# Moving the MLP's operands and the weight buffers within the SBUF partition of a two-layer trunk kernel

## The chip, the cores and the metric

The kernel runs on one core of one Trainium2 chip. The metric is device time in microseconds (us) of one execution; the median of three runs is quoted. The change alters no instruction, no size and no wait, only the addresses at which some buffers lie in each partition of the on-chip memory SBUF.

## The reference

Two layers over 512 tokens of width 1024, float32. Cut to what matters here:

```python
for l in range(2):
    z = rms_norm(x, g[0]) @ w_in[l]                 # 1024 x 3328: attention, gating unit, retention
    x = x + rms_norm(mix @ w_out[l], g[1])          # mix: the three head groups, from z
    # cross-attention into 256 memory tokens: x_wq, x_wkv, x_wo, all 1024 wide
    x = x + rms_norm(memory_attention(rms_norm(x, g[2]), mem_n, x_wq[l], x_wkv[l], x_wo[l]), g[3])
    h = rms_norm(x, g[4])
    f = jnp.square(jax.nn.relu(h @ w_up[l])) @ w_down[l]   # 1024 -> 4096 -> 1024
    x = x + rms_norm(f, g[5])
```

## The kernel before

Every large product is done on TensorE with three matmuls for one product of 128 x 128 by 128 x N: both operands are split into a high and a low part of type fp32r, and `three_passes` (L546 to L548) adds high*high, high*low and low*high into one PSUM tile of `proj`. The first operand of a matmul is the stationary one (loaded by an instruction of its own, LDWEIGHTS), the second one moves through the array, one column after another.

Weights come in blocks of four chunks of 128 rows by 512 columns (1 MB). SyncE loads a block into one of two slots of `w_raw` (L450, L512, L521), ScalarE copies it to `w_hi` (L905), VectorE subtracts to `w_lo` (L1149), and TensorE waits for `w_lo_done` before the block's first tile. `block_tile` then does, for each of the block's tiles, 4 chunks x 3 passes = 12 matmuls, in one of two modes:

- "tok": the activations are stationary and the weights move (output rows are tokens). Per layer: `va`, `qc`, `kc`, `vc`, `gc` with 384 columns; `uv`, `out0`, `out1`, `wo0`, `wo1` with 512 columns, 4 tiles each; `vm0`, `vm1` with 512 columns and 2 tiles.
- "feat": the weights are stationary and the activations move (output rows are features). Per layer: `qa`, `ka` (3 tiles of 512 columns), `qx0`, `qx1` (4 tiles of 512), `km0`, `km1` (4 tiles of 256).

Each job has 2 blocks. The activations of these jobs are `hT_hi`/`hT_lo` (normalised, transposed rows), for `km` and `vm` `memT_hi`/`memT_lo`. The MLP follows in four groups a layer, each `up0`, `up1` ("feat", from `hT` into `proj`, then relu, square and split into `uT_hi`/`uT_lo`, L1070, L1419, L1073, L1423) and `dn0`, `dn1` ("tok", `uT` stationary, 512 columns), 2 blocks of 4 tiles each. `first_up` does the first `up0` of a layer in two halves of 256 columns.

SBUF buffers are allocated in the order of the `sb(...)` calls, per partition: `xs`, `hT_hi`, `hT_lo`, `w_raw`, `w_hi`, `w_lo`, `ys` of 16 KiB each, `gains` 12, `hs` 8, `squares` 4, then some 15.5 KiB of small ones (`ident` first), then the arena of 56 KiB. Counted from the start of `xs`, `hT` lies at 16 to 48 KiB, the three weight buffers at 48 to 96 KiB, and the arena begins at 151.5 KiB. In the arena `part(name, kib, ...)` places buffers that take turns: among others `uT_hi` at 0, `uT_lo` at 16, `relu` at 32, `memT_hi` at 32 and `memT_lo` at 40 KiB, and the attention's rows.

Small products (scores, transposes by `ident`, retention) go into the PSUM tensor `work` in plain float32, between the tiles of the jobs.

Of the kernel before, what the change touches and what calls it, by code (L numbers as in the profile page):

```python
# [8 lines left out]
F32R = mybir.dt.float32r  # L9
# [7 lines left out]
P = 128  # L17
DEPTH, S, D, MEM = 2, 512, 1024, 256
# [13 lines left out]
KC = D // P  # L32
BK = 4
# [33 lines left out]
WSLOTS = 2  # L67
# [172 lines left out]
def trunk(nc, x, mem, positions, norm_g, w_in, sgu_w, sgu_b, sgu_ln_g, sgu_ln_b, w_out,  # L240
          x_wq, x_wkv, x_wo, w_up, w_down, c_ident, c_logcount, c_upper, c_decay, c_inv, out):
    weights = {"w_in": w_in, "w_out": w_out, "x_wq": x_wq, "x_wkv": x_wkv, "x_wo": x_wo}
    with ExitStack() as ctx:
        def sb(name, shape, dt=F32):
            return ctx.enter_context(nc.sbuf_tensor(name, shape, dt))
# [2 lines left out]
        xs = sb("xs", [P, T, D])  # L248
        hT_hi = sb("hT_hi", [P, KC, S], F32R)
        hT_lo = sb("hT_lo", [P, KC, S], F32R)  # L250
        w_raw = sb("w_raw", [P, WSLOTS, BK, 512])
        w_hi = sb("w_hi", [P, WSLOTS, BK, 512], F32R)
        w_lo = sb("w_lo", [P, WSLOTS, BK, 512], F32R)
        ys = sb("ys", [P, T, D])
        gains = sb("gains", [P, 3, D])
        hs_start = nc.sbuf_base
# [42 lines left out]
        gn_var = sb("gn_var", [P, NH])  # L299
        gn_ve = sb("gn_ve", [P, NH])  # L300
        gn_rstd = sb("gn_rstd", [P, NH])


        KIB = 1024
# [3 lines left out]
        def part(name, kib, shape, dt=F32):  # L308
            return nc.alloc_sbuf_tensor_at(name, shape, dt, offset=arena_start + int(kib * KIB))
# [26 lines left out]
                        "e3": part("half_squares3", 48, [P, T, 512], BF16)}  # L336
        half_squares["e2"] = half_squares["e1"]

        uT_hi = part("uT_hi", 0, [P, KC, S], F32R)
        uT_lo = part("uT_lo", 16, [P, KC, S], F32R)  # L340
        relu = part("relu", 32, [P, 2, S])

        proj = ctx.enter_context(nc.psum_tensor("proj", [P, 4, 512], F32))
# [196 lines left out]
        def _(pe):  # L540
# [9 lines left out]
            def block_tile(b_slot, kb, mode, t, moving, hi, lo, cols, at=0):  # L550

                for k in range(BK):
                    c = kb * BK + k
                    first, last = c == 0, kb == KB - 1 and k == BK - 1
                    if mode == "tok":
                        r = slice(t * P, (t + 1) * P)
                        mm = three_passes(proj[:, t, 0:moving], hi[:, c, r], lo[:, c, r],
                                          w_hi[:, b_slot, k, 0:cols], w_lo[:, b_slot, k, 0:cols], first, last)
                    else:
                        r = slice(t * P, (t + 1) * P)  # L560
                        tokens = slice(at, at + moving)
                        mm = three_passes(proj[:, t, tokens], w_hi[:, b_slot, k, r], w_lo[:, b_slot, k, r],
                                          hi[:, c, tokens], lo[:, c, tokens], first, last)
                return mm
# [233 lines left out]
            def first_up(l):  # L798


                late_slots = ((1, 0), (1, 1))
                for half in range(2):
                    turned_in(l, ("n3", 2 * half + 1))
                    for kb in range(KB):
                        b = HEAD_BLOCKS + kb
                        if half == 0:
                            pe.wait_ge(w_lo_done, nth(w_lo_done, l, b + 1))
                        for t in range(4):
                            if half == 0 and kb == 0:

                                pe.wait_ge(gained, nth(gained, l, GAINED["e2", 1, t] + 1))
                            mm = block_tile(b % WSLOTS, kb, "feat", t, S // 2, hT_hi, hT_lo, 512, at=half * (S // 2))
                            if half:
                                mm.then_inc(tile_done, 1)
                            if half == 0 and (kb, t) in late_slots:
                                turn_normed(l, "n3", 2 + late_slots.index((kb, t)))

            def mlp_group(l, g, jobs=GROUP_JOBS, last=False):
                for name in jobs:
                    i = GROUP_JOBS.index(name)  # L820
                    for kb in range(KB):
                        b = HEAD_BLOCKS + KB * i + kb
                        pe.wait_ge(w_lo_done, nth(w_lo_done, l, g * GROUP_BLOCKS + (b + 1)))
                        for t in range(4):
                            if kb == 0:

                                if name == "up0":
                                    pe.wait_ge(added, nth(added, l, g * UP_TILES + (t + 1 - T)))
                                elif name in ("up1", "dn0"):
                                    pe.wait_ge(emptied, nth(emptied, l, g * UP_TILES + (HEAD_TILES + 4 * (i - 1) + t + 1)))  # L830
                                else:
                                    pe.wait_ge(added, nth(added, l, g * UP_TILES + (t + 1)))
                            if name == "dn0" and t == 0:

                                pe.wait_ge(hidden_lo, nth(hidden_lo, l, g * UP_TILES + 4 * (kb + 1)))
                            if i < 2:
                                mm = block_tile(b % WSLOTS, kb, "feat", t, S, hT_hi, hT_lo, 512)
                            else:
                                mm = block_tile(b % WSLOTS, kb, "tok", t, 512, uT_hi, uT_lo, 512)
                            mm.then_inc(tile_done, 1)  # L840
                            if last and name == "dn0" and kb == 1 and t < MT:
                                turn_normed(l, "memk", t)
# [45 lines left out]
        def _(act):  # L888
# [196 lines left out]
            with act.Fori(0, DEPTH) as l:  # L1085
                for b in range(HEAD_BLOCKS):
                    if b < HEAD_BLOCKS - 1:
                        head_split(l, b + 1)
                    before_block(l, b)
                    tiles = JOBS[b // KB][5]  # L1090
                    if b < HEAD_BLOCKS - 1:
                        for t in range(tiles):
                            if b % KB == KB - 1:
                                empty(l, b, t)
                            after_tile(l, b, t)
                    if b == FIRST_BLOCK["qx1"] + 1:
                        for j in range(2, XUNITS - 2):
                            x_step(l, j)

                for what, t in N3_ACT:  # L1100
                    if what == "e":
                        empty(l, HEAD_BLOCKS - 1, t)
                    elif what == "x":
                        act.wait_ge(x_ready, nth(x_ready, l, BRANCHED["e2", t] + 1))
                        sum_squares(l, ("n3", t), xs[:, t])
                    elif what == "h":
                        turn_hi(l, ("n3", t), hT_hi, t)
                    else:
                        split_hi(l, HEAD_BLOCKS + t)
                with act.Fori(0, GROUPS - 1) as g:  # L1110
                    mlp_group(l, g, False)
                    split_hi(l, HEAD_BLOCKS + GROUP_BLOCKS + 1, g=g)
                mlp_group(l, GROUPS - 1, True)
# [3 lines left out]
        def _(dve):  # L1117
# [332 lines left out]
            with dve.Fori(0, DEPTH) as l:  # L1450
                links = itertools.count(1)
                for b in range(HEAD_BLOCKS):
                    if b < HEAD_BLOCKS - 1:
                        head_split(l, b + 1)
                    before_block(l, links, b)
                    if b == HEAD_BLOCKS - 1:
                        continue
                    for t in range(JOBS[b // KB][5]):
                        after_tile(l, links, b, t)
                    if b == FIRST_BLOCK["out0"]:  # L1460
                        for t in range(MT):
                            norm_mem(l, "memv", t)
                    if b == FIRST_BLOCK["qx1"] + 1:
                        for j in range(2, XUNITS - 2):
                            x_step(l, links, j)

                for what, t in N3_DVE:
                    if what == "e":
                        gain(l, "e2", 1, t)
                    elif what == "x":  # L1470
                        update(l, "e2", t)
                    elif what == "n":
                        norm(l, ("n3", t), xs[:, t])
                    elif what == "h":
                        turn_lo(l, ("n3", t), hT_hi, hT_lo, t)
                    else:
                        split_lo(l, HEAD_BLOCKS + t)
                with dve.Fori(0, GROUPS - 1) as g:
                    mlp_group(l, g, False)
                    split_lo(l, HEAD_BLOCKS + GROUP_BLOCKS + 1, g=g)  # L1480
                mlp_group(l, GROUPS - 1, True)
                assert next(links) == DVE_LINKS + 1
# [137 lines left out]
```

## Time and profile before

| | |
|---|---|
| median of three runs | 1605.96 us (1603.81 to 1606.32) |
| span of the profiled execution, first to last instruction | 1603.6 us |
| median less span: what lies around it | 2.3 us |
| TensorE busy | 98% of the span, 8008 matmuls |
| VectorE, ScalarE, GpSimd busy | 44%, 36%, 11% |
| chain of work that ended last | 91% on TensorE |

The page gives for each engine its busy share; a matmul's record is longer than its share of the engine, since matmuls overlap, so the rate of TensorE is read from the start times of successive matmuls and not from their durations. In the page's and the trace's names, `proj<-hT_hi,w_hi` is a matmul into `proj` whose moving operand is `hT_hi` and whose stationary operand is `w_hi`.

### The profile page before, as it was taken

The numbers are of one execution on the slowest core, as the hardware profiler recorded it, in microseconds if no ns is written. First come the engines' busy times: TensorE is split into PE (matmuls) and PEld (weight loads), VectorE is DVE, ScalarE is ACT, GpSimd is POOL, SyncE is SP. The second block draws the span as 40 slices with busy tenths as digits, with TensorE's granted clock in tenths as the row PEclk, the third lists the DMA queues.
The fourth block names the chain that finished last, engine by engine and source line by source line (L and its number), as shares of the span: only waits on it lengthen the run. The fifth ranks groups of instructions, "written<-read, shape, count | busy, mean of one in ns | idle before, by whom it ended". The sixth has DMA issues, their size and how long they took to land.

```text
span 1603.6 us, 21583 instructions
## 1 busy us (share of the span) xinstructions
PE 1567.5 (98%) x8008; PEld 1325.3 (83%) x8008; DVE 698.4 (44%) x840; ACT 575.3 (36%) x870; POOL 172.9 (11%) x195
## 2 busy tenths in 40 slices
PE   5999999999999999999999999999999999999997
PEld 5978798888888888888888788988888988888886
DVE  5323256624464342434571233656246433434345
ACT  5335333534343231313352443335344322232232
POOL 2001620300110000000030017102001100000001
PEclk9999999999999999999999999999999999999999
DMA  6332122431123322233333122125202323323332
GB/s 240 115 96 79 60 87 73 144 119 53 54 79 105 105 85 99 96 125 107 109 124 112 59 86 90 56 82 181 79 27 79 106 79 105 99 84 105 126 110 79
DMA packets 79966, 156.40 MB, mean 98 GB/s; under 512 B 3584, under 2 KB 19712, under 8 KB 79872
## 3 DMA queue, kind: packets, MB, share of 16 engines
q1 hardware_dynamic: 78000, 149.98, 28.3%
q10 hardware_dynamic: 1440, 3.56, 0.6%
q0 software_dynamic: 432, 1.57, 0.3%
q8 instruction: 62, 1.02, 0.3%
q14 instruction: 32, 0.26, 0.1%
HBM read 153.01 MB, written 2.10 MB: 97 GB/s over the span
## 4 chain that ended last, share of the span: by engine, by line
PE 91%; DVE 3%; issue 2%; ACT 2%; DMA 1%; POOL 0%; DVEq 0%; ACTq 0%; POOLq 0%; SPq 0%
PE proj L546 27%; PE proj L548 27%; PE proj L547 27%; PE work L595 2%; PE work L575 2%; PE work L611 1%; PE work L603 1%; PE work L729 1%; PE work L708 1%; PE work L683 1%; ACT w_hi L905 1%; DVE w_lo L1149 1%; DMA w_raw<-in_x_wkv_dram 1%; ACT x_probs L992 0%; DVE x_top L1331 0%
## 5 line engine op out<-in xcount | busy, mean ns | idle before, releaser
L1149 DVE TENSOR_TENSOR w_lo<-w_raw,w_hi 128x2048 fp32r<-128x2048 f32 (+1 forms) x137 | 301.3, 2199 | 487.6 <-ACT w_hi L905 484.9
L905 ACT ACTIVATE w_hi<-w_raw 128x2048 fp32r<-128x2048 f32 (+1 forms) x137 | 250.0, 1825 | 490.0 <-PE proj L548 483.9
L546 PE MATMUL proj<-hT_hi,w_hi 128*128 128x512 f32 (+1 forms) x800 | 298.9, 374 | 4.5 <-DVE w_lo L1149 4.5
L548 PE MATMUL proj<-hT_hi,w_lo 128*128 128x512 f32 (+1 forms) x800 | 297.9, 372 | 0.0
L547 PE MATMUL proj<-hT_lo,w_hi 128*128 128x512 f32 (+1 forms) x800 | 297.8, 372 | 0.0
L546 PE MATMUL proj<-w_hi,hT_hi 128*128 128x512 f32 (+1 forms) x640 | 240.5, 376 | 1.3 <-DVE hT_lo L1210 1.3
L548 PE MATMUL proj<-w_hi,hT_lo 128*128 128x512 f32 (+1 forms) x640 | 232.6, 363 | 0.0
L547 PE MATMUL proj<-w_lo,hT_hi 128*128 128x512 f32 (+1 forms) x640 | 231.9, 362 | 0.0
L546 PE MATMUL proj<-w_hi,uT_hi 128*128 128x512 f32 x512 | 202.8, 396 | 0.0
L548 PE MATMUL proj<-w_hi,uT_lo 128*128 128x512 f32 x512 | 202.6, 396 | 0.0
L547 PE MATMUL proj<-w_lo,uT_hi 128*128 128x512 f32 x512 | 202.5, 396 | 0.0
L546 PEld LDWEIGHTS proj<-hT_hi,w_hi 128*128 128x128 f32 x800 | 150.7, 188 | 31.2 <-DVE w_lo L1149 4.9
L548 PEld LDWEIGHTS proj<-hT_hi,w_lo 128*128 128x128 f32 x800 | 150.7, 188 | 26.3
L547 PEld LDWEIGHTS proj<-hT_lo,w_hi 128*128 128x128 f32 x800 | 150.7, 188 | 26.1
L546 PEld LDWEIGHTS proj<-w_hi,hT_hi 128*128 128x128 f32 x640 | 120.6, 188 | 13.5 <-issue 1.7
L548 PEld LDWEIGHTS proj<-w_hi,hT_lo 128*128 128x128 f32 x640 | 120.1, 188 | 12.8
L547 PEld LDWEIGHTS proj<-w_lo,hT_hi 128*128 128x128 f32 x640 | 120.6, 188 | 11.5
L548 PEld LDWEIGHTS proj<-w_hi,uT_lo 128*128 128x128 f32 x512 | 96.2, 188 | 23.2
L547 PEld LDWEIGHTS proj<-w_lo,uT_hi 128*128 128x128 f32 x512 | 96.2, 188 | 23.0
L546 PEld LDWEIGHTS proj<-w_hi,uT_hi 128*128 128x128 f32 x512 | 96.2, 188 | 23.0
L1506 POOL TENSOR_SCALAR half_mean<-half_sum 128x4 f32<-128x4 f32 x6 | 1.4, 233 | 921.2 <-ACT half_squares L919 921.2
L1432 DVE TENSOR_TENSOR ys<-proj,ys 128x512 f32<-128x512 f32 x64 | 44.0, 690 | 66.2 <-PE proj L548 65.5
(156 smaller groups left out, 1677.5 us busy)
## 6 DMA issues: line engine op xcount, KB each, us to landing
w_raw<-in_w_up_dram SPq DMA_DIRECT2D x32, 1024.0 KB, 5.4
w_raw<-in_w_down_dram SPq DMA_DIRECT2D x32, 1024.0 KB, 5.0
w_raw<-in_w_in_dram SPq DMA_DIRECT2D x28, 768.0 KB, 4.4
w_raw<-in_x_wkv_dram SPq DMA_DIRECT2D x17, 1024.0 KB, 5.1
w_raw<-in_w_out_dram SPq DMA_DIRECT2D x8, 1024.0 KB, 5.3
w_raw<-in_x_wq_dram SPq DMA_DIRECT2D x8, 1024.0 KB, 5.0
w_raw<-in_x_wo_dram SPq DMA_DIRECT2D x8, 1024.0 KB, 5.0
gains<-in_norm_g_dram SPq DMA_DIRECT2D x13, 512.0 KB, 6.0
```

Source lines behind the costliest of these rows:

```text
L546: nc.tensor.matmul(dst, l_hi, r_hi, start=first, stop=False)
L547: nc.tensor.matmul(dst, l_hi, r_lo, start=False, stop=False)
L548: return nc.tensor.matmul(dst, l_lo, r_hi, start=False, stop=last)
L575: mm = nc.tensor.transpose(work[:, 2 * (n % 2) + half, k * P:(k + 1) * P], src[:, c * P:(c + 1) * P], ident[:])
L595: nc.tensor.matmul(work[:, u % 2, 0:n], qaT[lo:lo + HD, h // 2, t * P:(t + 1) * P], kaT[lo:lo + HD, h // 2, 0:n], start=True, stop=True).t ...
L603: mm = nc.tensor.transpose(work[:, 2, j * P:(j + 1) * P], probs[:, u % 2, j * P:(j + 1) * P], ident[:])
L611: mm = nc.tensor.matmul(work[:, 3, h * HD:(h + 1) * HD], probsT[:, u % 2, j * P:(j + 1) * P], va[:, j, h * HD:(h + 1) * HD], start=(j == 0 ...
L683: mm = nc.tensor.matmul(work[:, 2, h * HD:(h + 1) * HD], innerT[:, h], vc[:, c, h * HD:(h + 1) * HD], start=(c == 0), stop=True, skip_grou ...
L708: mm = nc.tensor.matmul(work[:, u % 2, i * MEM:(i + 1) * MEM], qxT[:, c, t * P:(t + 1) * P], kmT[:, c, :], start=(k == 0), stop=(k == 1))
L905: nc.scalar.activation(w_hi[:, slot, :, 0:cols], w_raw[:, slot, :, 0:cols], ACT.Copy).then_inc(w_hi_done, 1)
L1149: nc.vector.tensor_tensor(w_lo[:, slot, :, 0:cols], w_raw[:, slot, :, 0:cols], w_hi[:, slot, :, 0:cols].bitcast(F32), ALU.subtract).then_i ...
L1432: nc.vector.tensor_tensor(part_y, proj[:, t], part_y, ALU.add).then_inc(added, 1)
```

## The change

The three weight buffers are allocated last, just ahead of the arena; the MLP's inner rows `uT` become the buffer `hT`; the third norm's rows, which `up0` and `up1` read, get a buffer of their own, `h3T`, in the place in the arena that `uT` had. All waits, instructions and sizes stay.

```diff
         hT_hi = sb("hT_hi", [P, KC, S], F32R)
         hT_lo = sb("hT_lo", [P, KC, S], F32R)
-        w_raw = sb("w_raw", [P, WSLOTS, BK, 512])
-        w_hi = sb("w_hi", [P, WSLOTS, BK, 512], F32R)
-        w_lo = sb("w_lo", [P, WSLOTS, BK, 512], F32R)
         ys = sb("ys", [P, T, D])
...
         gn_rstd = sb("gn_rstd", [P, NH])
+        w_raw = sb("w_raw", [P, WSLOTS, BK, 512])
+        w_hi = sb("w_hi", [P, WSLOTS, BK, 512], F32R)
+        w_lo = sb("w_lo", [P, WSLOTS, BK, 512], F32R)
...
-        uT_hi = part("uT_hi", 0, [P, KC, S], F32R)
-        uT_lo = part("uT_lo", 16, [P, KC, S], F32R)
+        h3T_hi = part("h3T_hi", 0, [P, KC, S], F32R)
+        h3T_lo = part("h3T_lo", 16, [P, KC, S], F32R)
+        uT_hi, uT_lo = hT_hi, hT_lo
...
-                            mm = block_tile(b % WSLOTS, kb, "feat", t, S // 2, hT_hi, hT_lo, 512, at=half * (S // 2))
+                            mm = block_tile(b % WSLOTS, kb, "feat", t, S // 2, h3T_hi, h3T_lo, 512, at=half * (S // 2))
...
-                                mm = block_tile(b % WSLOTS, kb, "feat", t, S, hT_hi, hT_lo, 512)
+                                mm = block_tile(b % WSLOTS, kb, "feat", t, S, h3T_hi, h3T_lo, 512)
...
-                        turn_hi(l, ("n3", t), hT_hi, t)
+                        turn_hi(l, ("n3", t), h3T_hi, t)
...
-                        turn_lo(l, ("n3", t), hT_hi, hT_lo, t)
+                        turn_lo(l, ("n3", t), h3T_hi, h3T_lo, t)
```

Counted from the start of `xs`, `hT` stays at 16 to 48 KiB and the arena at 151.5 KiB; `ys` and all that follows it move down by 48 KiB; `w_raw` is then at 103.5, `w_hi` at 119.5 and `w_lo` at 135.5 KiB, ending where the arena begins.

## Rows read from the trace of the kernel before

**Rows 1.** The page's parts 1 (engines) and 4 (chain, by engine).
```profile
PE 1567.5 (98%) x8008; PEld 1325.3 (83%) x8008; DVE 698.4 (44%) x840; ACT 575.3 (36%) x870; POOL 172.9 (11%) x195
...
PE 91%; DVE 3%; issue 2%; ACT 2%; DMA 1%; POOL 0%; DVEq 0%; ACTq 0%; POOLq 0%; SPq 0%
```
**Rows 2.** Waits of TensorE, whole span: total us, times, longest us.
```profile
PE work L575 <- DVE hs L1180: 14.6, 1, 14.6
PE proj L546 <- DVE w_lo L1149: 7.4, 4, 2.8
```
**Rows 3.** Timeline, TensorE, up0/up1 then dn0/dn1 of one group: start us, us.
```profile
539.54 0.39 PE L546 MATMUL proj<-hT_hi,w_hi 128*128 128x512 f32 x1
...
582.84 0.40 PE L548 MATMUL proj<-hT_hi,w_lo 128*128 128x512 f32 x1
583.07 0.39 PE L546 MATMUL proj<-w_hi,uT_hi 128*128 128x512 f32 x1
...
627.63 0.40 PE L548 MATMUL proj<-w_hi,uT_lo 128*128 128x512 f32 x1
```
**Rows 4.** Those two stretches by windows: us, PE, PEld, DVE, ACT, POOL, clock, DMA.
```profile
539.50:583.00 43.50, 43.50 (x193) 36.03 (x192) 18.23 (x18) 14.98 (x17) 0.00 (x0) 1.00 0.30 97
583.00:627.80 44.80, 44.80 (x193) 36.08 (x193) 15.82 (x14) 9.29 (x7) 0.00 (x0) 1.00 0.29 94
```
**Rows 5.** Timeline, TensorE: out1; va; second half of the first up0.
```profile
275.90 0.39 PE L546 MATMUL proj<-w_hi,hT_hi 128*128 128x512 f32 x1
...
297.44 0.40 PE L548 MATMUL proj<-w_hi,hT_lo 128*128 128x512 f32 x1
...
49.68 0.34 PE L546 MATMUL proj<-w_hi,hT_hi 128*128 128x384 f32 x1
...
66.16 0.33 PE L548 MATMUL proj<-w_hi,hT_lo 128*128 128x384 f32 x1
...
467.19 0.28 PE L546 MATMUL proj<-hT_hi,w_hi 128*128 128x256 f32 x1
...
472.83 0.28 PE L548 MATMUL proj<-hT_hi,w_lo 128*128 128x256 f32 x1
```
**Rows 6.** Timeline, TensorE: first block of vm0, layer 0.
```profile
297.67 0.39 PE L546 MATMUL proj<-w_hi,memT_hi 128*128 128x512 f32 x1
...
303.03 0.40 PE L548 MATMUL proj<-w_hi,memT_lo 128*128 128x512 f32 x1
```
**Rows 7.** Timeline, TensorE: first block of km1, layer 1, from its second matmul.
```profile
825.95 0.28 PE L547 MATMUL proj<-memT_lo,w_hi 128*128 128x256 f32 x1
...
831.32 0.28 PE L548 MATMUL proj<-memT_hi,w_lo 128*128 128x256 f32 x1
```
**Rows 8.** TensorE's groups by form, whole span: count, busy us, mean ns.
```profile
L546 PE MATMUL proj<-w_hi,uT_hi 128*128 128x512 f32 x512 | 202.8, 396 | 0.0
```
**Rows 9.** The same view: transposes by ident, stationary operand in two places.
```profile
L716 PE MATMUL work<-ident,x_probs 128*128 128x128 f32 x64 | 9.7, 274 | 0.2
...
L575 PE MATMUL work<-ident,ys 128*128 128x128 f32 x64 | 8.3, 273 | 0.0
```
**Rows 10.** ScalarE's and VectorE's groups by form: into hT and into the arena.
```profile
L932 ACT ACTIVATE hT_hi<-work 128x512 fp32r<-128x512 f32 x64 | 34.6, 594 | 32.6 <-PE work L575 32.6
...
L932 ACT ACTIVATE memT_hi<-work 128x512 fp32r<-128x512 f32 x20 | 11.0, 596 | 10.6 <-PE work L575 10.6
...
L1210 DVE TENSOR_TENSOR hT_lo<-work,hT_hi 128x512 fp32r<-128x512 f32 x64 | 40.8, 684 | 6.9 <-ACT hT_hi L932 6.9
...
L1210 DVE TENSOR_TENSOR memT_lo<-work,memT_hi 128x512 fp32r<-128x512 f32 x20 | 12.7, 683 | 4.2 <-ACT memT_hi L932 4.2
```
**Rows 11.** The same view: the two splitting operations of a block.
```profile
L905 ACT ACTIVATE w_hi<-w_raw 128x2048 fp32r<-128x2048 f32 x109 | 208.4, 1912 | 454.8 <-PE proj L548 448.7 <-DMA w_raw<-in_x_wkv_dram 6.0
...
L1149 DVE TENSOR_TENSOR w_lo<-w_raw,w_hi 128x2048 fp32r<-128x2048 f32 x109 | 249.8, 2292 | 400.6 <-ACT w_hi L905 398.2 <-issue 1.8 <-DVE yc L1311 0.5
```
**Rows 12.** DMA issues by line: count, KB each, median us to landing.
```profile
w_raw<-in_w_up_dram SPq DMA_DIRECT2D x32, 1024.0 KB, 5.4
```

## The prediction, made before the changed kernel was run

> **What bounds the kernel now.** I read the page's busy shares and its chain first. TensorE is busy 98% of the span and the chain of work that ended last is 91% TensorE [rows 1]. The waits of TensorE say the same from the other side: 14.6 us once, at the start, before there is anything to multiply, then 7.4 us in four waits for split weights, and next to nothing else [rows 2]. So for nearly the whole span the time is the number of matmuls times the distance between their starts. Nothing in the change alters the number. What can change is the distance, and whether that depends on the place of the operands can be read in this trace, because the kernel already uses several pairs of places.
>
> The view for that is the timeline of TensorE, first and last start of an undisturbed run of matmuls, divided by the intervals between them. A matmul of N columns at the full clock takes N/2.4 ns of array time; the granted clock in both MLP stretches is 1.00, so 2.4 GHz [rows 4]. What is left over per matmul I call the overhead. I call "near" what lies in the first 96 KiB counted from `xs` (`hT`, and before the change the weights) and "far" what lies in the arena, from 151.5 KiB on.
>
> - Weights stationary near, `hT` moving near, 512 columns (`up`): 192 matmuls, 539.54 to 582.84, 43.30/191 = 226.7 ns, overhead 13.4 [rows 3].
> - `hT` stationary near, weights moving near (`out1`): 96 matmuls, 21.54/95 = 226.7 ns, overhead 13.4; `va`, 384 columns: 16.48/95 = 173.5 ns, overhead 13.5; half of an `up0`, 256 columns, 48 matmuls: 5.64/47 = 120.0 ns, overhead 13.3 [rows 5]. Width and mode do not matter.
> - `uT` stationary far, weights moving near (`dn`): 192 matmuls, 583.07 to 627.63, 44.56/191 = 233.3 ns, overhead 20.0 [rows 3]. `memT` stationary far, weights moving near (`vm0`): 24 matmuls, 5.36/23 = 233.0 ns, 19.7 [rows 6].
> - Weights stationary near, `memT` moving far (`km1`), 256 columns: 47 matmuls, 5.37/46 = 116.7 ns, overhead 10.1 [rows 7].
>
> A stationary operand that lies far thus costs 6.6 ns a matmul, a moving operand that lies far gives 3.3 ns back. That the 6.6 ns belong to the place and not to the down projection is shown by `vm0`, another stage with another load, and by `up` next to `dn`, where the other engines are if anything busier in the faster stretch (VectorE 18.2 against 15.8 us, ScalarE 15.0 against 9.3) [rows 4].
>
> The Trainium skill speaks against any effect. "TensorE: Matmul & The Clock Gate", section "Back-to-back issue gap", gives a gap of N/2.4 + 2.5 ns at the full clock, with no word of where the operands lie, and "SBUF — State Buffer", section "Who interferes with whom", gives TensorE two independent read ports that never wait on anyone. By these pages the change would be worth nothing. The trace disagrees in both respects: 13.4 ns and not 2.5, and 20.0 where the stationary operand is far.
>
> **The change part by part.** The moved weights lie at 119.5 to 151.5 KiB, in a stretch that no fp32r operand uses before, between near and far. I take them as far, since they end where the arena begins; the other case is priced below. Matmul counts are for both layers: jobs x 2 blocks x tiles x 4 chunks x 3 passes x 2.
>
> 1. Head jobs with `hT` stationary: 5 jobs of 384 and 5 of 512 columns, 1920 matmuls, from near/near to moving far: 1920 x -3.3 = -6.3 us.
> 2. `qa`, `ka`, `qx0`, `qx1`: 672 matmuls, weights stationary go far, `hT` moving stays near: 672 x +6.6 = +4.4 us.
> 3. `dn`: 1536 matmuls (512 of each of the three passes [rows 8]), stationary comes near, moving goes far: from 20.0 to 10.1, 1536 x -9.9 = -15.2 us.
> 4. `up`: 1344 matmuls of 512 and 384 of 256 columns, from near/near to far/far. No matmul of this kind has both operands far before. Bounds: 10.1, if only the moving place counted, and 20.0, if only the stationary place counted. Between them the two effects could add (13.4 + 6.6 - 3.3 = 16.7), or only a difference of places could matter (13.4, as when both are near). I take 13.4: near/near is the nearest row, for it too has both operands in one region, and it is alike in both modes although their places swap. Change: 0.
> 5. `km`: 384 matmuls from moving far to far/far, +3.3 each: +1.3 us. `vm`: 192 from stationary far to far/far, -6.6 each: -1.3 us.
>
> Sum: -6.3 + 4.4 - 15.2 + 0 + 1.3 - 1.3 = -17.1 us. With d for the ns by which far/far exceeds near/near, it is -17.1 + 2.304 d (1344 + 384 + 384 + 192 = 2304 matmuls), from -24.7 us at d = -3.3 to -1.9 us at d = 6.6.
>
> The second unknown is the -3.3. It is known at 256 columns alone; for 512 columns it lies between 0 and the full mirror of the stationary effect, -6.6. Overheads did not change with width near/near, so I take -3.3; at -6.6 for 384 and 512 columns steps 1 and 3 become -12.7 and -20.3 us.
>
> What else moves costs nothing that I can find. ScalarE and VectorE write `hT` and the arena in the same time, 594 against 596 and 684 against 683 ns [rows 10]. `h3T` and `uT` are written by the same instructions in the same order under the same waits. Loading (5.4 us [rows 12]) and splitting (1.9 and 2.3 us [rows 11]) together take 9.6 us and are spread over two slots, beside blocks of 48 x 0.227 = 10.9 us; a block at 223.4 ns a matmul is 10.7 us long, so the cover stays. ScalarE's idle time ahead of the split is almost all waiting for TensorE [rows 11]. If that cover were gone, each late block would stall TensorE. `ident` goes near, and 232 transposes (64 of `x_probs`, 120 of `probs`, 48 of `qkc`) keep a far stationary operand; at 6.6 ns that is +1.5 us. I take 0, since transposes last 274 ns with `x_probs` stationary, deep in the arena, and 273 with `ys`, which began at 96 KiB [rows 9]; the bound goes into the range, on both sides.
>
> The profiled execution would so take 1603.6 - 17.1 = 1586.5 us; with the 2.3 us around it the median goes from 1605.96 to 1588.9 us.
>
> **The rivals.**
>
> - The effects add (d = 3.3): -17.1 + 7.6 = -9.5 us, 1596.5. For it: two effects, each seen alone. Against: nothing here.
> - The moving effect is -6.6 at 384 and 512 columns: -12.7 + 4.4 - 20.3 + 1.3 - 1.3 = -28.6 us, 1577.4. For it: the neat symmetry with +6.6; against: the only row says 3.3.
> - The border lies beyond the moved weights, so they count as near: `dn` -6.6 x 1536 = -10.1, `up` with only the moving operand far -3.3 x 1728 = -5.7, nothing else: -15.8 us, 1590.2.
> - Slower: the stationary operand alone decides, and the 3.3 ns of the moving one are a matter of 256 columns. Then step 1 gives nothing, `dn` -10.1, step 2 +4.4, `up` 1728 x 6.6 = +11.4, `km` 384 x 9.9 = +3.8, `vm` 0: +9.5 us, 1615.5. Without the moving effect it is slower from d = 2.5 ns on (2304 d = 5.7 us). For it: the stationary effect is seen at 512 columns in two stages, and the moving effect rests on one job; against: `km1` has the far moving operand cheaper, not equal.
> - Nothing happens, or next to it: `dn`'s 6.6 ns come from something else than place: 1606.0. (This is also what the two pages of the Trainium skill named above would give.) The case d = 6.6 with the moving effect intact, 1604.1, goes with it. Against: the `vm0` row.
>
> **How the numbers follow.** Forecast 1588.9: 0.42; adding 0.22; the larger moving effect 0.16; weights near 0.05; nothing 0.07; slower 0.08. A measurement of this kernel can tell about 0.2%, 3.2 us, from no change. Faster by more than that are the first four, 0.85; within it 0.07; slower 0.08. The range leaves out the last two, 0.15, and reaches from 1577.4 less the 1.5 us of the transposes to 1596.5 plus that bound and 2 us for a value of d between 3.3 and 6.6: 1576 to 1600.
>
> **What the profile after would show.** `dn` at 223.4 ns from start to start, `up` still 226.7 (230.0 if the effects add, 233.3 if the stationary alone decides), `out1` 223.4 and `va` 170.2, `qx1` 233.3, `km1` 120.0, `vm0` 226.7; transposes at 273 to 274 ns; no new wait of TensorE for `w_lo`. The prediction falls if `up` is slower by more than 4 ns, if `dn` does not go below `up`, or if TensorE shows new waits.

## The result and the profile after

The changed kernel takes 1613.81 us (1612.78 to 1614.36) against 1605.51 us of the kernel before on the same chip, a ratio of 1.005 with a 95% interval of 1.0038 to 1.0063: slower by about 0.5%, where 1.0% faster was forecast. The span of the profiled execution went from 1603.6 to 1611.7 us. TensorE is as busy as before; the page's parts 1 and 4 of the changed kernel answer to [rows 1]:

```profile
PE 1574.4 (98%) x8008; PEld 1322.7 (82%) x8008; DVE 698.4 (43%) x840; ACT 575.6 (36%) x870; POOL 173.6 (11%) x195
...
PE 92%; DVE 3%; issue 2%; ACT 2%; DMA 1%; POOL 0%; DVEq 0%; ACTq 0%; POOLq 0%; SPq 0%
```

The largest wait besides the one at the start grew by 1 us (compare [rows 2]):

```profile
PE proj L547 <- DVE w_lo L1150: 8.4, 4, 2.4
```

So the time came from the distance between the starts of the matmuls. The timeline of TensorE after the change, first and last matmul of the runs that answer to [rows 3] (`up`, then `dn`), [rows 5] (`out1`, `va`), [rows 6] (`vm0`) and [rows 7] (`km1`), and of `qx1`; columns are start in us, length in us, then the matmul:

```profile
545.72 0.39 PE L547 MATMUL proj<-h3T_hi,w_hi 128*128 128x512 f32 x1
...
589.02 0.40 PE L549 MATMUL proj<-h3T_hi,w_lo 128*128 128x512 f32 x1
589.25 0.39 PE L547 MATMUL proj<-w_hi,hT_hi 128*128 128x512 f32 x1
...
633.82 0.39 PE L549 MATMUL proj<-w_hi,hT_lo 128*128 128x512 f32 x1
...
278.11 0.39 PE L547 MATMUL proj<-w_hi,hT_hi 128*128 128x512 f32 x1
...
300.28 0.39 PE L549 MATMUL proj<-w_hi,hT_lo 128*128 128x512 f32 x1
...
50.23 0.34 PE L547 MATMUL proj<-w_hi,hT_hi 128*128 128x384 f32 x1
...
66.69 0.34 PE L549 MATMUL proj<-w_hi,hT_lo 128*128 128x384 f32 x1
...
348.63 0.40 PE L547 MATMUL proj<-hT_hi,w_hi 128*128 128x512 f32 x1
...
359.59 0.40 PE L549 MATMUL proj<-hT_hi,w_lo 128*128 128x512 f32 x1
...
829.58 0.28 PE L548 MATMUL proj<-memT_lo,w_hi 128*128 128x256 f32 x1
...
835.09 0.28 PE L549 MATMUL proj<-memT_hi,w_lo 128*128 128x256 f32 x1
...
300.50 0.39 PE L547 MATMUL proj<-w_hi,memT_hi 128*128 128x512 f32 x1
...
305.72 0.39 PE L549 MATMUL proj<-w_hi,memT_lo 128*128 128x512 f32 x1
```

The same run of `qx1` before the change:

```profile
345.41 0.39 PE L546 MATMUL proj<-hT_hi,w_hi 128*128 128x512 f32 x1
...
356.06 0.39 PE L548 MATMUL proj<-hT_hi,w_lo 128*128 128x512 f32 x1
```

Divided by the number of intervals, in ns:

| run (intervals) | before | forecast | after |
|---|---|---|---|
| `up` (191) | 226.7 | 226.7 | 43.30/191 = 226.7 |
| `dn` (191) | 233.3 | 223.4 | 44.57/191 = 233.4 |
| `out1` (95) | 226.7 | 223.4 | 22.17/95 = 233.4 |
| `va`, 384 columns (95) | 173.5 | 170.2 | 16.46/95 = 173.3 |
| `qx1` (47) | 226.6 | 233.3 | 10.96/47 = 233.2 |
| `km1`, 256 columns (46) | 116.7 | 120.0 | 5.51/46 = 119.8 |

`vm0` went to 227.0 (300.50 to 305.72 over 23 intervals), as forecast. All these runs of 512 columns fit one sentence: a matmul costs 226.7 ns when both operands are in the same group of buffers (`hT` and the old weights; the arena and the moved weights), and 233.3 when they are not, whichever of the two is where. At 384 columns the mixed pair costs nothing here, at 256 it is 3 ns cheaper.

The stages of a layer, as distances between the first matmuls of the jobs, sum up the same way: `qa` and `ka` 33.15 to 34.02 us, `uv` 29.10 to 29.48, the four jobs of 384 columns 121.83 to 121.81, `out0` and `out1` 47.26 to 48.32, `vm` 25.94 to 25.66, `qx` with the first attention steps 64.04 to 65.31, `wo` 58.06 to 58.85. That is +4.1 us, and the second layer gives +4.2, together 8.2 us, where the span grew by 8.1. So close an agreement is partly luck, because the stages left out of the sum also moved and happened to cancel. The MLP from the first `up1` on went from 333.98 to 334.32 in the first layer. `km0` and `km1` took 0.7 us longer there and 2.6 us less in the second layer, and the first layer's first `up0` took 1.6 us longer. The two large differences have little to do with the addresses. TensorE first stood still for 2.2 to 2.8 us in these stages, waiting for `w_lo`. In some of the executions it then ran for a while at the lower level of its clock, 1.2 GHz, where a matmul of 256 columns takes 213 ns. In `km0` of the second layer this happened before the change and not after it (first row before, second row after; the granted clock is the number behind the brackets, 0.52 against 1.00):

```profile
815.60:821.90 6.30, 6.28 (x30) 6.28 (x31) 4.77 (x3) 1.62 (x3) 5.58 (x6) 0.52 0.48 169
821.80:825.00 3.20, 3.14 (x26) 3.14 (x27) 2.12 (x3) 1.32 (x3) 2.85 (x4) 1.00 0.49 154
```

In the first layer's `up0` it was the other way round, with 0.50 after the change (458.50 to 461.30 us) and 1.00 before it (453.90 to 456.20 us). The other profiled runs have such stretches too, now in one of these stages and now in the other.

### The profile page after: what moved, and what is told of

Its sections match the earlier page's. It is cut to its first block, busy times and chain, and to the rows that moved or that the text cites. A ratio compares the mean times of both kernels' runs of the same rounds, so it can differ in the third digit from the quotient of the medians.

```text
span 1611.7 us, 21583 instructions
## 1 busy us (share of the span) xinstructions
PE 1574.4 (98%) x8008; PEld 1322.7 (82%) x8008; DVE 698.4 (43%) x840; ACT 575.6 (36%) x870; POOL 173.6 (11%) x195
## 4 chain that ended last, share of the span: by engine, by line
PE 92%; DVE 3%; issue 2%; ACT 2%; DMA 1%; POOL 0%; DVEq 0%; ACTq 0%; POOLq 0%; SPq 0%
PE proj L547 27%; PE proj L548 27%; PE proj L549 27%; PE work L596 2%; PE work L576 2%; PE work L612 1%; PE work L604 1%; PE work L730 1%; PE work L709 1%; PE work L684 1%; DVE w_lo L1150 1%; DMA w_raw<-in_x_wkv_dram 1%; ACT x_probs L993 0%; DVE x_top L1332 0%; PE work L663 0%
## 5 line engine op out<-in xcount | busy, mean ns | idle before, releaser
L547 PE MATMUL proj<-w_hi,hT_hi 128*128 128x512 f32 (+1 forms) x1152 | 445.1, 386 | 1.3 <-DVE hT_lo L1211 1.3
L548 PE MATMUL proj<-w_lo,hT_hi 128*128 128x512 f32 (+1 forms) x1152 | 436.1, 379 | 0.0
L549 PE MATMUL proj<-w_hi,hT_lo 128*128 128x512 f32 (+1 forms) x1152 | 436.1, 379 | 0.0
L547 PEld LDWEIGHTS proj<-w_hi,hT_hi 128*128 128x128 f32 x1152 | 216.5, 188 | 38.5 <-issue 1.8
L547 PE MATMUL proj<-h3T_hi,w_hi 128*128 128x512 f32 (+1 forms) x576 | 211.6, 367 | 4.7 <-DVE w_lo L1150 4.7
L549 PE MATMUL proj<-h3T_hi,w_lo 128*128 128x512 f32 (+1 forms) x576 | 211.1, 366 | 0.0
L548 PE MATMUL proj<-h3T_lo,w_hi 128*128 128x512 f32 (+1 forms) x576 | 211.0, 366 | 0.0
L547 PEld LDWEIGHTS proj<-h3T_hi,w_hi 128*128 128x128 f32 x576 | 109.1, 189 | 22.8 <-DVE w_lo L1150 5.1
L549 PEld LDWEIGHTS proj<-h3T_hi,w_lo 128*128 128x128 f32 x576 | 109.2, 190 | 17.5
L548 PEld LDWEIGHTS proj<-h3T_lo,w_hi 128*128 128x128 f32 x576 | 109.2, 190 | 17.3
```

The source lines that it names most:

```text
L547: nc.tensor.matmul(dst, l_hi, r_hi, start=first, stop=False)
L548: nc.tensor.matmul(dst, l_hi, r_lo, start=False, stop=False)
L549: return nc.tensor.matmul(dst, l_lo, r_hi, start=False, stop=last)
```

## The experiments

Addresses in this section are bytes from the start of the partition. In the kernel before, the built program has `hT_hi` at 32,896, `w_hi` at 82,048 and the arena at 171,680; after the change `w_hi` is at 138,912. The arena's start is only rounded up to a multiple of 32. So the two groups of the result differ in place, and they also differ in the remainder of their addresses: modulo 256, `hT` and the old weights have 128, the arena and the moved weights 160. Two theories thus fit both traces, place and remainder.

**A map of places.** A bare kernel, all of whose matmuls have a new stationary operand:

```diff
+            def group(i, s, m, n, bits=False, at=0):
+                for r in range(REPS):                      # 16 of each kind
+                    j = (r % 4) * P
+                    w = tiles[s][:, j + at:j + at + P] if j + at + P <= 512 else tiles[s][:, 0:P]
+                    mv = tiles[m][:, 0:n]
...
+                    mm = nc.tensor.matmul(ps[:, i % 4, 0:n], w, mv, start=(r == 0), stop=(r == REPS - 1))
```

> Not the kernel but a bare sequence of fp32r matmuls on an otherwise idle core, 16 of each kind, every one with a new stationary operand; nothing of the reference is computed. Buffers are named by their distance in KiB from the start of the partition (xs starts at 16.1 KiB there, so the old weights end at 112.1, the moved w_hi begins at 135.7, the arena at 167.7). Theory of the mismatch: in the changed kernel 512-column matmuls take 226.7 ns from start to start with both operands on one side and 233.3 ns with one on each side, whichever it is; so with the stationary operand at 20 the sweep of the moving operand gives 226.7 up to a border between 112 and 136 KiB and 233.3 beyond it, with the stationary operand at 216 the opposite, and with the stationary operand at 108 the same as at 20. By width the mismatch costs 6.6 ns at 512, 0 at 384, and gives 3.3 back at 256. Theory of distance: what counts is how far the operands are from each other (over about 70 KiB), so the step in the sweep moves with the stationary operand: from 20 it comes at about 90 to 94, from 108 nearly nowhere, from 216 at about 146. Theory of load: the 6.6 ns need the other engines or DMAs beside TensorE; then every kind takes 226.7 here.

Place does nothing. With the stationary operand at 20, 216 or 108 KiB and the moving one at 25 places between 22 and 214 KiB, with the places of the two swapped, and in steps of 2 KiB from 100 to 144 KiB, every kind has the same length (four runs at 512 columns that follow one of 448 columns apart, which begin irregularly). Runs at 64 to 448 columns, with both operands low, both high, or one of each, don't differ by place either: 120.0 ns at 256 columns and 173.3 at 384 in all four cases. From the timeline of this kernel (`ps<-a206k,a020k`: moving operand at 206 KiB, stationary at 20; x16: sixteen matmuls, from the start of the first to the end of the last):

```profile
163.61 3.79 PE L67 MATMUL ps<-a206k,a020k 128*128 128x512 f32 x16
...
170.86 3.79 PE L67 MATMUL ps<-a022k,a216k 128*128 128x512 f32 x16
...
603.77 3.89 PE L67 MATMUL ps<-a040k,a020k 128*128 128x512 f32 x16
```

3.79 us less the last one's 0.39 over 15 intervals is 226.7 ns. The last row is the exception that told where to look: both operands are in the lower part, but here three of every four slices of the stationary operand began 32 bytes later (`at=8`), and (3.89 - 0.39)/15 = 233.3 ns. All buffers of this map began on multiples of 1024 bytes, so with equal remainders neither place nor distance costs anything. The load of other engines isn't needed for the slow pace either, since 233.3 ns came on an idle core.

**One part alone: the MLP's buffers.** The changed kernel with the weights back where they were:

```diff
         hT_lo = sb("hT_lo", [P, KC, S], F32R)
+        w_raw = sb("w_raw", [P, WSLOTS, BK, 512])
+        w_hi = sb("w_hi", [P, WSLOTS, BK, 512], F32R)
+        w_lo = sb("w_lo", [P, WSLOTS, BK, 512], F32R)
         ys = sb("ys", [P, T, D])
...
         gn_rstd = sb("gn_rstd", [P, NH])
-        w_raw = sb("w_raw", [P, WSLOTS, BK, 512])
-        w_hi = sb("w_hi", [P, WSLOTS, BK, 512], F32R)
-        w_lo = sb("w_lo", [P, WSLOTS, BK, 512], F32R)
```

> The MLP's part of the change alone: inner rows in hT, third norm's rows in the arena, the weights stay where they were. Mismatch theory: up with 512 columns gets one operand on each side, 1344 x 6.6 = +8.9 us; its halves of 256 columns 384 x -3.3 = -1.3; dn has both near, 1536 x -6.6 = -10.1; together -2.5, some 1603.0 us, up at 233.3 ns from start to start and dn at 226.7. The theory of the prediction (a far stationary operand costs 6.6, a far moving one gives 3.3 back at every width) wants up at 223.4, dn at 226.7 and 1589.7 us.

Measured: 1605.38 us against 1605.88, ratio 0.9996 (0.9986 to 1.0005), no difference. Both expected times were missed, that of the mismatch theory (1603.0) by 2.4 us. The timeline has `up1` from its first matmul to its last (95 intervals) at 22.16/95 = 233.3 ns and `dn` (191) at 43.33/191 = 226.9:

```profile
563.11 0.39 PE L547 MATMUL proj<-h3T_hi,w_hi 128*128 128x512 f32 x1
...
585.27 0.40 PE L549 MATMUL proj<-h3T_hi,w_lo 128*128 128x512 f32 x1
585.51 0.40 PE L547 MATMUL proj<-w_hi,hT_hi 128*128 128x512 f32 x1
...
628.84 0.39 PE L549 MATMUL proj<-w_hi,hT_lo 128*128 128x512 f32 x1
```

The penalty has only changed sides: what `dn` gained, `up` lost. The forecast's theory, 223.4 for `up`, falls. Of the 2.4 us a part lies in the two first `up0`: their matmuls of 256 columns did become 3 ns cheaper, but the stages took 28.5 us in place of 27.3, with a stretch of 213 ns a matmul in each that the kernel before doesn't have there.

**One part alone: the weights.** The three `sb` lines move as in the change, the MLP's buffers stay as they were.

```diff
         hT_lo = sb("hT_lo", [P, KC, S], F32R)
-        w_raw = sb("w_raw", [P, WSLOTS, BK, 512])
-        w_hi = sb("w_hi", [P, WSLOTS, BK, 512], F32R)
-        w_lo = sb("w_lo", [P, WSLOTS, BK, 512], F32R)
...
         gn_rstd = sb("gn_rstd", [P, NH])
+        w_raw = sb("w_raw", [P, WSLOTS, BK, 512])
+        w_hi = sb("w_hi", [P, WSLOTS, BK, 512], F32R)
+        w_lo = sb("w_lo", [P, WSLOTS, BK, 512], F32R)
```

> The weights' part of the change alone: the three weight buffers just ahead of the arena, the MLP's rows where they were (hT for up, the arena for dn). Mismatch theory: up gets one operand on each side (weights far, hT near), +8.9 at 512 columns; dn has both far, -10.1; the head jobs as in the changed kernel, where they cost about +9 in all; together about +8 less 1.3 for the 256-column halves if both mismatches are alike there: 1612 us, up at 233.3 ns, dn at 226.7. The theory of the prediction: dn at 230.0 or 226.7, out1 at 223.4, up at 233.3.

Measured: 1613.42 us, ratio 1.0054 (1.0038 to 1.0071), `up1` 22.16/95 = 233.3 ns, `dn` 43.32/191 = 226.8:

```profile
565.32 0.40 PE L546 MATMUL proj<-hT_hi,w_hi 128*128 128x512 f32 x1
...
587.48 0.40 PE L548 MATMUL proj<-hT_hi,w_lo 128*128 128x512 f32 x1
587.72 0.39 PE L546 MATMUL proj<-w_hi,uT_hi 128*128 128x512 f32 x1
...
631.04 0.39 PE L548 MATMUL proj<-w_hi,uT_lo 128*128 128x512 f32 x1
```

The loss of the whole change is that of the weights' part, in the head jobs; in the MLP it trades one mixed pair for another. Both runs fit place as well as remainder.

**Another remainder for the arena.** The kernel before with the arena 96 bytes further up:

```diff
-        arena_start = -(-nc.sbuf_base // 32) * 32
-        ctx.enter_context(nc.sbuf_tensor("arena", [P, ARENA_KIB * KIB // 4], F32))
+        arena_start = -(-nc.sbuf_base // 128) * 128
+        ctx.enter_context(nc.sbuf_tensor("arena", [P, ARENA_KIB * KIB // 4 + 24], F32))
```

> The kernel before with the arena moved up by 96 bytes, from an address of 32 to one of 0 modulo 128, like hT and the weights before; nothing else. In before and after alike, the operands that disagree in place also disagree in this alignment (hT and the old weights 0 modulo 128, arena and moved weights 32), so alignment would explain both traces as well as place. Alignment theory: dn drops from 233.3 to 226.7 ns, vm too, about -11 us, 1594.5. Mismatch-of-place theory: no change, 1605.5, dn at 233.3.

Measured: 1605.58 us, ratio 0.9998 (0.9988 to 1.0008). Taken alone this speaks for place and against alignment. But `dn` was not quite the same: 44.40/191 = 232.5 ns where it had been 233.3 [rows 3].

```profile
585.01 0.40 PE L546 MATMUL proj<-w_hi,uT_hi 128*128 128x512 f32 x1
...
629.41 0.40 PE L548 MATMUL proj<-w_hi,uT_lo 128*128 128x512 f32 x1
```

The arena's new address, 171,776, is a multiple of 128 like 32,896 and 82,048, but modulo 256 it has 0 and they have 128. I had chosen the modulus too small, and the test had replaced one disagreement by another. Since place had fallen by the map, I took the remainder modulo something larger than 128.

**A map of remainders.** Twenty-four matmuls of each kind, buffers on chosen remainders:

```diff
+        sta = {o: nc.alloc_sbuf_tensor_at(f"s{o:04d}b", [P, 512], F32R, offset=20480 + i * step + o)
+               for i, o in enumerate(OFFSETS)}            # step = 4096
+        mov = {o: nc.alloc_sbuf_tensor_at(f"m{o:04d}b", [P, 512], F32R, offset=118784 + i * step + o)
+               for i, o in enumerate(OFFSETS)}
```

> A bare sequence of fp32r matmuls again, 24 of each kind, nothing of the reference computed. Stationary and moving buffers lie on addresses of a chosen remainder modulo 4096 (s0160b: 160 bytes past a multiple, m0000b: on one). Theory of the phase: what costs is that the addresses of the two operands have different remainders, modulo some power of two that is at least 512 or 256; equal remainders give 226.7 ns at 512 columns whatever the remainder; a difference of 32 gives about 233.3 and one of 128 about 232.4, at 256 columns 116.7 to 119.3 in place of 120.0, at 384 173.3 either way. Theory of the stationary operand alone: s0032b and the like cost 7 ns, a shifted moving operand nothing; then equal remainders of 160 cost 7 ns too.

From its timeline (`m0032b,s0000b`: the moving operand's address has the remainder 32, the stationary one's 0):

```profile
53.57 5.63 PE L71 MATMUL ps<-m0000b,s0000b 128*128 128x512 f32 x24
59.04 5.77 PE L71 MATMUL ps<-m0032b,s0000b 128*128 128x512 f32 x24
...
75.76 5.76 PE L71 MATMUL ps<-m0128b,s0000b 128*128 128x512 f32 x24
...
98.17 5.63 PE L71 MATMUL ps<-m0256b,s0000b 128*128 128x512 f32 x24
...
164.57 5.75 PE L71 MATMUL ps<-m0000b,s0032b 128*128 128x512 f32 x24
...
269.99 5.63 PE L71 MATMUL ps<-m0032b,s0032b 128*128 128x512 f32 x24
...
302.90 3.04 PE L71 MATMUL ps<-m0000b,s0000b 128*128 128x256 f32 x24
...
319.98 2.89 PE L71 MATMUL ps<-m0192b,s0000b 128*128 128x256 f32 x24
...
394.71 4.40 PE L71 MATMUL ps<-m0160b,s0000b 128*128 128x384 f32 x24
...
449.26 4.32 PE L71 MATMUL ps<-m0000b,s0096b 128*128 128x384 f32 x24
```

At 512 columns a difference of 0 or 256 bytes has the short length, 32 or 128 the long one, in either direction, and 32 against 32 is short again. (The first few intervals after a change of kind are irregular, so the 24 give a little more than the steady pace.) From the single starts, without the first three intervals:

- 512 columns, moving operand ahead by 0 modulo 256: 226.7 to 227.8 ns, and 226.7 in all of them once the start has died away; by 64: 228.8; by 32, 128, 192 or 224: 233.3; by 96: 233.4 to 234.0; by 160: 234.3 to 234.4. The pattern repeats with 256 bytes.
- 384 columns: equal remainders 173.3, the others 173.3 to 176.7. Here the difference alone doesn't decide. The moving operand is 160 bytes ahead modulo 256 in both of the last two rows above, and the paces are 176.7 and 173.3 ns. The pair of `va` after the change (stationary 128, moving 160) has 176.7 in the map and 173.3 in the kernel, so at this width the map doesn't carry over.
- 256 columns: equal remainders 119.5 to 120.0, a difference of 32 in either direction 116.7 to 118.2, the moving operand 192 ahead 113.4. The pair of `km1` before (stationary 128, moving 160) has 116.7, as `km1` had [rows 7].

One value at 512 columns is not settled by remainders modulo 256. The pair 128 and 256 has 232.4 in either direction, as `dn` had with the arena 96 bytes further up (232.5), but 128 against 0 has 233.3, although it has the same remainders. The runs don't show what makes this 1 ns.

**One remainder for all, in both kernels.** The 32 bytes of a small buffer are allocated first, so that `hT` has the arena's remainder:

```diff
+        exp_table = sb("exp_table", [P, 1])
         xs = sb("xs", [P, T, D])
...
-        exp_table = sb("exp_table", [P, 1])
```

In the kernel before:

> The kernel before, with the 32 bytes of exp_table allocated ahead of xs in place of near the end: hT and the weights move up by 32 bytes, so that they have the remainder 160 modulo 512, as the arena, which stays. No other change. Theory of the phase: dn and vm from 233.3 to 226.7 ns (1536 + 192 matmuls, -11.4 us), km from 116.8 to 120.0 (+1.2): 1595.5 us. Theory that the place counts: no change, 1605.7.

Measured: 1595.49 us (1594.91 to 1595.92) against 1605.57, ratio 0.9939 (0.9923 to 0.9956), where 1595.5 had been expected; `dn` 43.29/191 = 226.6 ns.

```profile
580.67 0.39 PE L546 MATMUL proj<-w_hi,uT_hi 128*128 128x512 f32 x1
...
623.96 0.39 PE L548 MATMUL proj<-w_hi,uT_lo 128*128 128x512 f32 x1
```

In the changed kernel:

> The changed kernel with the same move of exp_table: hT goes to the remainder 160 modulo 512, which the moved weights and the arena have. Places far and near are as in the changed kernel. Theory of the phase: out0, out1, uv, wo0, wo1, qa, ka, qx0, qx1 and dn at 226.7 ns (some 3170 matmuls of 512 columns less 6.6 each, -21 us), but they were partly above that level before for other reasons: 1595 us, the same as the other kernel with one phase, so that the place costs nothing. Theory that the place counts: no change, 1613.8.

Measured: 1596.91 us (1595.80 to 1598.31), ratio to the kernel before 0.9949 (0.9933 to 0.9966); `dn` 43.30/191 = 226.7 ns, `out1` 21.53/95 = 226.6.

```profile
276.18 0.39 PE L547 MATMUL proj<-w_hi,hT_hi 128*128 128x512 f32 x1
...
297.71 0.39 PE L549 MATMUL proj<-w_hi,hT_lo 128*128 128x512 f32 x1
...
581.84 0.39 PE L547 MATMUL proj<-w_hi,hT_hi 128*128 128x512 f32 x1
...
625.14 0.39 PE L549 MATMUL proj<-w_hi,hT_lo 128*128 128x512 f32 x1
```

Thirty-two bytes take 17 us off the changed kernel and 10 us off the one before. The weights lie beside `hT` in the one kernel and just ahead of the arena in the other, and still the undisturbed runs of 512 columns (`up`, `dn`, `out1`) have 226.7 ns in both. Whether the 1.4 us between the two kernels are real is open: the times hardly overlap (1595.80 to 1595.92 is common to both), the intervals of the ratios do. The first of the two is the best version of this study, better than before and after.

**A middle value.** The map has one difference of middling cost. The kernel before with the arena 160 bytes further up, which makes the weights 64 ahead of `uT` and `memT`:

```diff
-        arena_start = -(-nc.sbuf_base // 32) * 32
-        ctx.enter_context(nc.sbuf_tensor("arena", [P, ARENA_KIB * KIB // 4], F32))
+        arena_start = -(-nc.sbuf_base // 32) * 32 + 160
+        ctx.enter_context(nc.sbuf_tensor("arena", [P, ARENA_KIB * KIB // 4 + 40], F32))
```

> The kernel before with the arena 160 bytes further up, so that uT and memT have the remainder 64 modulo 256 and hT and the weights 128: the moving operand is 64 ahead in dn and vm, and 64 behind (192) in km. Nothing else moves. Theory of the phase with the values of the map: dn and vm 228.8 ns in place of 233.3, 1728 x -4.5 = -7.8 us, km 113.4 in place of 116.8, -1.2 us: 1596.6 us. Theory that only equal and unequal remainders count: no change, 1605.6. Theory of the place: no change.

Measured: 1598.18 us (1596.39 to 1598.61), ratio 0.995 (0.9933 to 0.9966); `dn` 43.72/191 = 228.9 ns:

```profile
583.49 0.39 PE L546 MATMUL proj<-w_hi,uT_hi 128*128 128x512 f32 x1
...
627.21 0.39 PE L548 MATMUL proj<-w_hi,uT_lo 128*128 128x512 f32 x1
```

The value read on the bare kernel holds in the full one to 0.1 ns, and the time follows within 1.6 us. `km1` followed in part. Its first block, in the first layer and then in the second, from the second matmul to the last:

```profile
36.82 0.28 PE L547 MATMUL proj<-memT_lo,w_hi 128*128 128x256 f32 x1
...
42.24 0.28 PE L548 MATMUL proj<-memT_hi,w_lo 128*128 128x256 f32 x1
...
821.15 0.28 PE L547 MATMUL proj<-memT_lo,w_hi 128*128 128x256 f32 x1
...
826.37 0.28 PE L548 MATMUL proj<-memT_hi,w_lo 128*128 128x256 f32 x1
```

That is 5.42/46 = 117.8 ns in the one and 5.22/46 = 113.5 in the other, with the same operands at the same addresses, and either pace is kept to the end of its block. So at 256 columns the addresses alone don't fix the pace: the matmuls can settle on one of two. What decides between them isn't shown.

**Finer steps.**

> A third bare sequence of fp32r matmuls, nothing of the reference computed: remainders in steps of 4 to 16 bytes, slices of the stationary operand 0 to 512 bytes apart, widths of 400 to 508 columns. The map before it shows 226.7 ns where the remainders modulo 256 agree, 228.8 where the moving operand is 64 ahead, some 233.4 elsewhere. Theory of the phase: this goes on at finer steps, with nothing below 226.7 at 512 columns; slices of the stationary operand that are not a multiple of 256 bytes apart lose the 226.7. Rival, that the 13.3 ns above N/2.4 are themselves a collision that another remainder avoids: some fine remainder gives 220 ns or less, which would be worth 6 ns x 5700 matmuls = 35 us.

From its timeline:

```profile
39.70 10.62 PE L66 MATMUL ps<-m0004b,s0004b 128*128 128x512 f32 x44
...
244.49 5.76 PE L66 MATMUL ps<-m0000b,s0000b 128*128 128x512 f32 x24
...
304.92 5.12 PE L66 MATMUL ps<-m0000b,s0000b 128*128 128x448 f32 x24
309.87 4.96 PE L66 MATMUL ps<-m0064b,s0000b 128*128 128x448 f32 x24
```

Nothing at 512 columns is below 226.6 ns. The rival that a lucky remainder avoids the 13.3 ns as well finds no support in what was tried. (Its price of 35 us counted the matmuls of 384 columns too; 6 ns on the 4704 of 512 columns would be 28 us.) Four things are new.

- At steps below 32 bytes the difference alone doesn't decide. With the stationary operand at 0 and the moving one 4 to 24 bytes ahead it is 228.8 to 240.0 ns in no order by size (4 ahead 236.7, 8 ahead 233.2, 12 ahead 228.8), and 28, 240 and 252 ahead are as good as 0. With the moving operand at 0 and the stationary one at 252, the moving one is 4 ahead as well, and the pace is 226.7; with the stationary one at 28 it is 235.0.
- Equal remainders are not enough when they are 4: (10.62 - 0.40)/43 = 237.7 ns.
- The slices of the stationary operand matter. At 0, 256 or 512 bytes from one slice to the next it is 226.7 ns; at 128 bytes (second row) 233.3, at 64, 32 and 16 between 230.9 and 232.2, at 448 and 480 it is 230.3 and 230.0.
- Equal remainders are not the best at every width. At 448 columns they have 206.7 ns, 20.0 above N/2.4, and the moving operand 64 bytes ahead has 200.2 (the last two rows). At 496 columns it is the other way round, 223.3 against 226.7.

## Why the prediction was wrong

- **What bounds the kernel** was right. TensorE's start-to-start distance set the time, the only new wait was 0.9 us for `ys`, and the stages with changed distances add up to 8.2 us, where the span grew by 8.1.
- **"A stationary operand that lies far thus costs 6.6 ns a matmul, a moving operand that lies far gives 3.3 ns back"** is the step that failed. The paces were read rightly; the cause was not. Near and far differed in the trace in a second respect, the remainder modulo 256, and I had not compared the addresses, only the places. In the map of places no place costs anything. That `vm0` and `up` next to `dn` confirm the place did not follow: they rule out the stage and the load, but `vm0` has the same remainders as `dn`. And the two numbers are not the effects of two operands: both are the cost of one thing, the remainders 128 and 160 in place of equal ones, at two widths. In the kernel it is +6.6 ns at 512 columns, 0 at 384, and -3.3 at 256.
- **"Overheads did not change with width near/near, so I take -3.3"** carried this into the sum. It was read at 256 columns alone, on one job, and used for 3456 matmuls of 384 and 512. With equal remainders the overhead is indeed the same at 256, 384 and 512 columns (though not at 448, where it is 20.0 ns); with unequal ones it is not, so the row could not be extended.
- **Step 1** (-6.3 us) became 0 at 384 columns and a loss at 512: 2 x (0.38 + 1.06 + 0.79) = +4.5 us by the stages. The full 960 x 6.6 = 6.3 us is not reached: `out1`, an unbroken run, lost 0.62 us a layer, while `uv`, `out0`, `wo0` and `wo1`, with small products between their tiles, lost 0.39 to 0.44. In `uv` the six intervals after such an interruption grew by 2.8 ns only and the later ones by 6.2, because the kernel before needs several matmuls (224 to 236 ns each) to find back to 226.7.
- **Step 2** was right: +4.4 forecast, 2 x (0.87 + 1.27) = +4.3 by the stages, for another reason.
- **Step 3** (-15.2 us) was the largest error: 0. `dn` was a pair of unequal remainders before (stationary 160, moving 128) and is one after (128 and 160).
- **Steps 4 and 5**: `up` at 226.7 ns was forecast, as were `km1` and `vm0`. The choice that both operands in one group is like both in the other held, but for another reason: their remainders are equal.
- **The slower rival** gave 1615.5, close to 1613.81, but its mechanism, `up` at 233.3, `dn` at 226.7 and step 1 at nothing, did not occur: `up` was untouched and step 1 was where half of the loss came from. The time was near for a wrong reason.
- **The rival "nothing happens"** had the right thought, that the 6.6 ns of `dn` come from something else than place, at a chance of 0.07. Its time of 1606.0 did not come, because moving the weights also changed their remainder.
- **The skill's rule.** The page "TensorE: Matmul & The Clock Gate" of the Trainium skill, section "Back-to-back issue gap", gives N/2.4 + 2.5 ns, 215.8 ns at 512 columns, for a single matmul, and names no address. The runs show 226.7 to 240.0 ns for the same matmul on bare kernels at a granted clock above 0.99, with nothing but the addresses changed; the measurement decides. The page says nothing of place, and in the map place costs nothing.
- **What else moves** cost nothing, as forecast: VectorE 698.4 and ScalarE 575.6 us busy against 698.4 and 575.3 [rows 1].

With the cause as the runs show it, the sum would have been: 960 matmuls of "tok" and 672 of "feat" with 512 columns from equal to unequal remainders, `va` and the other jobs of 384 columns unchanged, `dn` unequal in both, `up` equal in both, `vm` -6.6 and `km` +3.3 ns each: 6.3 + 4.4 - 1.3 + 1.3 = +10.7 us at most, for 8.3 measured.

What stays open is why 256 bytes, why 13.3 ns remain at best at 512 columns, and what decides at widths where the difference alone doesn't; the runs show the dependence, not the circuit behind it. Only fp32r matmuls were mapped over remainders, each map in one execution.

## What to carry to other kernels

When a trace shows two paces for one shape of matmul, compare the full addresses of the operands, not only their regions, before moving anything; in a kernel that TensorE bounds, giving all operands of fp32r matmuls one remainder modulo 256 (160, by moving 32 bytes) was worth 0.6%, where the rearrangement of the regions and its two parts gave nothing or a loss. This holds for matmuls of mostly 512 columns; at 256 and 448 columns another pair was faster than equal remainders. An effect read at one width should be measured at the width where it is to be used, with a bare sequence of matmuls if the kernel has no such pair. And a test that changes one disagreement into another (128 for 32 here) looks like a test that found nothing; the small shift it did cause, 0.8 ns in `dn`, was the useful part of it.

## What the runs showed of the hardware

- The distance between fp32r matmuls of 512 columns with a new stationary operand each follows the difference of the two operands' addresses modulo 256 bytes, if both are multiples of 32: 226.7 ns at a difference of 0, 228.8 when the moving operand is 64 ahead, 232.4 to 234.4 otherwise. The full kernel shows 226.7, 228.9, 232.5 and 233.3.
- At steps of 4 bytes both addresses matter, not their difference alone: 226.7 to 240.0 ns, and 237.7 where both have the remainder 4. At 384 columns this is so at multiples of 32 as well, with 173.3 and 176.7 ns at the same difference.
- At equal remainders the distance does not depend on where in the partition the operands lie, in steps of 8 KiB from 22 to 214 KiB.
- At 256 columns equal remainders are not the best: they have 119.5 to 120.0 ns, a difference of 192 has 113.4. In the full kernel that pair settled on 113.5 ns in one block and on 117.8 in another.
- After a change of operands or a small product in between, several matmuls of 512 columns with equal remainders take 224 to 236 ns before 226.7 is reached, in full and bare kernels alike.
